# Attention heads taken two at a time, on the two halves of the array, in a three-block transformer kernel

## Time and profile before

| what | value |
|---|---|
| median of 3 runs | 1319.49 us (1318.44 to 1320.66) |
| the profiled execution, its own time | 1322.08 us |
| its span, first to last instruction | 1320.3 us |
| mean granted TensorE clock | 0.963 of 2.4 GHz |
| TensorE busy | 1267.0 us (96%) |
| VectorE busy | 850.8 us (64%) |
| ScalarE busy | 547.3 us (41%) |

### The profile page before, as it was taken

The page is one execution under the profiler, slowest core; times in us unless marked ns, Lnnn a source line. Parts: engine busy times, 40 slices in busy tenths (PEclk is TensorE's granted clock), DMA queues, the critical chain, the costliest instruction groups (busy, mean ns, idle before and its releaser), DMA issues.

```text
span 1320.3 us, 17461 instructions
## 1 busy us (share of the span) xinstructions
PE 1267.0 (96%) x7032; PEld 1074.1 (81%) x7032; DVE 850.8 (64%) x1314; ACT 547.3 (41%) x683; POOL 35.3 (3%) x43
## 2 busy tenths in 40 slices
PE   7999999999998999999999999989999999999996
PEld 5788777887997877777899888987877877999885
DVE  4565455446677788766777554675878766677542
ACT  5555454343433344443444333432344443434331
POOL 1121000000000000000000000000000000000000
PEclk9999999799998799999999999997899999999999
DMA  8456544236443322344455555452223444455540
GB/s 283 168 188 223 200 143 135 98 106 242 179 157 134 114 103 103 128 160 161 158 189 172 202 193 191 160 195 96 97 96 112 143 160 160 157 173 181 207 159 32
DMA packets 39468, 206.56 MB, mean 156 GB/s; under 512 B 4003, under 2 KB 13731, under 8 KB 16307
## 3 DMA queue, kind: packets, MB, share of 16 engines
q1 hardware_dynamic: 39052, 205.22, 44.7%
q10 hardware_dynamic: 336, 0.22, 0.1%
HBM read 204.23 MB, written 1.20 MB: 156 GB/s over the span
## 4 chain that ended last, share of the span: by engine, by line
PE 84%; DVE 9%; DVEq 2%; ACT 2%; issue 1%; DMA 0%; POOL 0%; POOLq 0%; ACTq 0%
PE panel L832 17%; PE panel L834 16%; PE panel L833 16%; PE panel L855 6%; PE panel L854 6%; PE panel L853 6%; PE tile L883 4%; DVE ring_parts L559 3%; PE heads_out L1034 2%; DVE area L1918 2%; PE tile L1161 1%; PE tile L1160 1%; DVEq L1919 1%; PE tile L1088 1%; PE tile L1086 1%
## 5 line engine op out<-in xcount | busy, mean ns | idle before, releaser
L559 DVE TENSOR_TENSOR ring_parts<-ring,ring_high 128x2048 fp32r<-128x2048 f32 (+1 forms) x185 | 415.3, 2257 | 169.3 <-ACT ring_high L534 151.5
L534 ACT ACTIVATE ring_high<-ring 128x2048 fp32r<-128x2048 f32 (+1 forms) x185 | 348.2, 1887 | 272.0 <-PE panel L834 205.0
L832 PE MATMUL panel<-ring_high,hT_high 128*128 128x512 f32 (+2 forms) x688 | 290.7, 423 | 11.6 <-DVE ring_parts L559 9.2
L834 PE MATMUL panel<-ring_high,hT_low 128*128 128x512 f32 (+2 forms) x688 | 272.4, 396 | 0.0
L833 PE MATMUL panel<-ring_parts,hT_high 128*128 128x512 f32 (+2 forms) x688 | 271.6, 395 | 0.0
L853 PE MATMUL panel<-hT_high,ring_high 128*128 128x256 f32 x704 | 199.4, 283 | 0.0
L855 PE MATMUL panel<-hT_high,ring_parts 128*128 128x256 f32 x704 | 199.2, 283 | 0.0
L854 PE MATMUL panel<-hT_low,ring_high 128*128 128x256 f32 x704 | 199.2, 283 | 0.0
L832 PEld LDWEIGHTS panel<-ring_high,hT_high 128*128 128x128 f32 x688 | 134.4, 195 | 55.8 <-issue 34.1
L832 PE MATMUL panel<-ring_high,area_parts 128*128 128x512 f32 x384 | 153.4, 399 | 5.0 <-DVE tok L1789 5.0
L834 PEld LDWEIGHTS panel<-ring_high,hT_low 128*128 128x128 f32 x688 | 134.0, 195 | 28.7
(11 more groups left out here) (225 smaller groups left out, 1256.3 us busy)
## 6 DMA issues: line engine op xcount, KB each, us to landing
ring<-in_w_layers_dram SPq DMA_DIRECT2D x140, 1024.0 KB, 4.9
ring<-in_w_first_dram SPq DMA_DIRECT2D x40, 1024.0 KB, 4.9
area<-bias_rows SPq DMA_DIRECT2D x16, 160.0 KB, 2.9
ring<-in_w_layers_dram SPq DMA_DIRECT2D x4, 560.0 KB, 3.8
area<-bias_rows SPq DMA_DIRECT2D x16, 96.0 KB, 2.9
area<-bias_rows SPq DMA_DIRECT2D x1, 1536.0 KB, 8.5
area<-in_gains_dram SPq DMA_DIRECT2D x3, 512.0 KB, 5.7
x<-in_x_dram SPq DMA_DIRECT2D x2, 512.0 KB, 4.3
```

The lines of the kernel that those rows point to most:

```text
L534: act.activation(ring_hi[:, hi, 0:w], ring[:, slot, 0:w], ACT.Copy).then_inc(high_ready, 1)
L559: g.tensor_tensor(ring_lo[:, slot, 0:w], ring[:, slot, 0:w], ring_hi[:, hi, 0:w], ALU.subtract).then_inc(low_ready, 1)
L832: pe.matmul(ps[:, b, 0:width], high, hi[:, k, :], start=first, stop=False)
L834: mm = pe.matmul(ps[:, b, 0:width], low, hi[:, k, :], start=False, stop=last)
```

## The change

Units are ordered in pairs of heads that lie on different halves of the array: in branch A and in the second blocks the order of heads becomes `PAIRS = [0, 4, 1, 5, 2, 6, 3, 7]`; in branch B neighbours already alternate. A score step now takes a pair, and in branch B one group g of it: the matmuls of the two heads alternate, into two PSUM tiles. The order of steps becomes: scores of the first pair; then for each pair T, T, scores of the next pair, V, V, and in the layers one empty slot. ScalarE's exponentials of unit u+2 stand at V(u). The columns of `heads_out`, the gates and outputs are addressed in the new order of heads, and the bias loads of the first block follow the pairs.

```diff
 def units_first():
-    return [("A", h, 1) for h in range(H)] + [("B", h, 2) for h in range(H)]
+    return [("A", h, 1) for h in PAIRS] + [("B", h, 2) for h in range(H)]
 def units_layer():
-    return [("s", h, 1) for h in range(H)] + [("w", h, 1) for h in range(H)]
+    return [("s", h, 1) for h in PAIRS] + [("w", h, 1) for h in PAIRS]
-def unit_steps(n):
-    out = [("S", 0)]
-    for u in range(n):
-        if u + 1 < n:
-            out.append(("S", u + 1))
-        out += [("T", u), ("V", u)]
+def pair_steps(units, spare):
+    def scores(p):
+        return [("S", p, g) for g in range(units[2 * p][2])]
+    pairs = len(units) // 2
+    out = scores(0)
+    for p in range(pairs):
+        out += [("T", 2 * p), ("T", 2 * p + 1)]
+        if p + 1 < pairs:
+            out += scores(p + 1)
+        out += [("V", 2 * p), ("V", 2 * p + 1)] + [None] * spare
     return out
-FIRST_PLAN = make_plan(FIRST_WIDE, unit_steps(2 * H), range(KC), {("mg2", 3): ["yA"]})
-LAYER_PLAN = make_plan(LAYER_WIDE, unit_steps(2 * H), (0, 1, 2, 3, 4, 5, 7), {
+FIRST_PLAN = make_plan(FIRST_WIDE, pair_steps(units_first(), 0), range(KC), {("mg2", 3): ["yA"]})
+LAYER_PLAN = make_plan(LAYER_WIDE, pair_steps(units_layer(), 1), (0, 1, 2, 3, 4, 5, 7), {
...
 # TensorE, first block
+            def scores_first(p, g):
+                pair = units[2 * p:2 * p + 2]
+                outs = [tile_for(part, score_tile(unit, g)) for unit in pair]
+                for b in range(NB):
+                    if pair[0][0] == "A":
+                        for i, (_, h, _) in enumerate(pair):
+                            r, c = head_rows(h)
+                            mm[i] = pe.matmul(outs[i][0][:, to], qaT[r, c, bs], kaT[r, :], start=True, stop=True)
...
 # TensorE, second blocks
+                        for i, (_, h, _) in enumerate(pair):
+                            r, c = head_rows(h)
+                            pe.matmul(outs[i][0][:, 0:P], qT[r, c, 0:P], kT[r, w, 0:P], start=True, stop=True)
+                        for i, (_, h, _) in enumerate(pair):
+                            r, c = head_rows(h)
+                            pe.matmul(outs[i][0][:, P:3 * P], qT[r, c, P:TOKENS], kT[r, w, :], start=True, stop=True)\
+                              .then_inc(outs[i][1], 1)
...
 # ScalarE (exp_layer likewise)
-                elif e == "S" and u == 0:
-                    exp_first(0)
+                elif e == "S":
+                    if u == 0:
+                        exp_first(0)
+                        exp_first(1)
-                elif e == "V" and u + 1 < len(units):
-                    exp_first(u + 1)
+                elif e == "V" and u + 2 < len(units):
+                    exp_first(u + 2)
...
 # VectorE
                 if e == "S":
-                    logits_first(u)
+                    for i in range(2):
+                        logits_group(2 * u + i, g)
...
 # sum_out, by b and in the new order of columns
-                e = v.tensor_tensor(y, y, two("yc").rearrange("p (b n) -> p b n", b=2)[:, :, hs_], ALU.add)
+                for b in range(NB):
+                    to = heads_of_group(y[:, b, :], i)
+                    e = v.tensor_tensor(to, to, heads_of_group(yc[:, b, :], i), ALU.add)
...
 # SyncE: bias of a pair of heads
-                            sp.dma_start(Es[odd:P:2, n % 2, i * TOEP:(i + 1) * TOEP], head_bias("A", 2 * n + i, odd))\
+                            sp.dma_start(Es[odd:P:2, n % 2, i * TOEP:(i + 1) * TOEP], head_bias("A", n + 4 * i, odd))\
```

More of the change, by code:

```diff
@@ L42 @@
 HALF = 4 * 512
+PAIRS = [0, 4, 1, 5, 2, 6, 3, 7]
 SLOTS = 6
@@ L145, in make_plan @@
             if s in slots and steps:
-                at.append(steps.pop(0))
+                step = steps.pop(0)
+                if step:
+                    at.append(step)
             plan[p, s] = at + [(e, 0) for e in extra.get((p, s), [])]
@@ L162, in plan_tiles @@
     for steps in plan.values():
-        for e, u in steps:
-            if e in "ST":
-                out += [f"{e}{units[u][0]}{units[u][1]}{g}" for g in range(units[u][2])]
+        for e, u, *g in steps:
+            if e == "S":
+                out += [score_tile(units[2 * u + i], g[0]) for i in range(2)]
+            elif e == "T":
+                out += [f"T{units[u][0]}{units[u][1]}{g}" for g in range(units[u][2])]
             elif e == "cmpS":
@@ L839, in rows_out @@
                         if plan:
-                            for e, u in plan[name, 4 * i + k]:
-                                step(e, u)
+                            for e in plan[name, 4 * i + k]:
+                                step(*e)
                         if 4 * i + k in after:
@@ L967, in head_rows @@
                 return slice(s, s + HD), h % 4
[L969 to L970 removed]
+            def scores_first(p, g):
+                pair = units[2 * p:2 * p + 2]
+                outs = [tile_for(part, score_tile(unit, g)) for unit in pair]
+                mm = [None, None]
                 for b in range(NB):
[L972 to L982, removed]
[L983 to L984 removed]
@@ L996, in turn_outputs, with step_first @@
                     turn(part, f"{('yA', 'yB')[t]}{b}", lambda c: y[:, b, c * P:(c + 1) * P])
-            def step_first(e, u):
+            def step_first(e, u, g=0):
+                if e == "S":
+                    if u == g == 0:
+                        for p in NORMED:
+                            for b in range(NB):
+                                wait_evicted(part, f"{p}{b}")
+                    scores_first(u, g)
+                    return
                 kind, h, n = units[u]
@@ new lines, in logits_group @@
+                mx, load = mxs[u % 2], bias_of(u)
+                if g == 0:
+                    v.wait_ge(E_loaded[load % 2], 64 * (load // 2 + 1) if kind == "A" else 32 * (load // 2 + 3))
+                    if u >= 2:
+                        k2, h2, n2 = units[u - 2]
+                        for g2 in range(n2):
+                            tile_of(v, part, f"T{k2}{h2}{g2}")
+                ps = tile_of(v, part, score_tile(units[u], g))
+                for b in range(NB):
+                    init = first[:, 12 + h:13 + h] if kind == "A" else low
+                    if g == 0:
+                        at = backwards(P * (1 - b), TOKENS, end=TOEP * (1 + (u % 2 if kind == "A" else 0)))
+                    else:
+                        at = backwards(0, TOKENS, end=5 * P)
+                    e = v.tensor_tensor_reduce(L[:, b, g * TOKENS:(g + 1) * TOKENS], ps[:, b * TOKENS:(b + 1) * TOKENS],
+                                               Es[:, load % 2, at], 1.0, init, ALU.add, ALU.max, mx[:, b, g:g + 1])
```

160 lines of the change are left out of this document (86 added, 74 removed).

## The result

| | before | after |
|---|---|---|
| median of the runs | 1318.97 us (4 runs, 1313.19 to 1320.66) | 1282.07 us (4 runs, 1281.08 to 1289.99) |
| the profiled execution | 1322.08 us | 1282.98 us |
| its span | 1320.3 us | 1281.2 us |
| mean granted clock | 0.963 | 0.975 |

The ratio is 0.974, 95% interval 0.969 to 0.979. The forecast was 1291 in a range of 1281 to 1304: right in sign and mechanism, 9 us too high, and one us from the range's lower end. The profiled executions differ by 39.1 us where the sum said 28.5. One kernel's time varies from execution to execution with the clock that it is granted: 49 more executions of the kernel before, made beside the experiments, took 1312.5 to 1323.0 us (median 1317.7), and ten of the kernel after 1281.0 to 1290.0 (median 1283.3), so that the medians differ by 34.4 and the profiled pair, with a slow one of before, by more.

What follows compares the result with a forecast made beforehand. TensorE was taken as the bound, busy 96%, with VectorE next in the layers. Terms summing to -28.5 took the profiled 1322.1 us to 1293.6; less 2.6 to the median, 1291 us, range 1281 to 1304.

Steps and rivals of the forecast that it cites:

- Points 1 to 3: Score steps taken in pairs: 5.0 us less in branch A, 7.0 in branch B, 16.8 less 1.8 in the layers.
- Points 4 and 5: Branch B: V10's 3.0 us wait for ScalarE goes, and the 13.66 us at half clock behind it, 6.3 us less.
- Point 6: First T, one chunk behind first scores, waits: 1.4 us in branch A, 2.4 and 1.0 in layers; 4.8 back.
- Point 7: VectorE in the layers, around the retention's normalisation: TensorE waits more for it, together 3.0 us back.
- does not come back: Rival: the low-clock stretch of branch B appears elsewhere, one or two more than forecast: 1297 to 1303 us; chance 0.18.
- one less: Rival: one low-clock stretch fewer, in the layers: 1285 us, or to 1281 with fewer waits; chance 0.08.
- Staggered starts: Rival: matmuls start in program order, so each score step lasts one instruction longer, 5.5 us: 1296 us; chance 0.08.
- One after the other: Rival: array halves do not overlap when both are wide, a pair saves only 0.40 us: 1308 us; chance 0.08.
- Late pairs: Rival: pairs' probabilities come late in the layers, TensorE waits at each pair's first T, 34 us: 1325 us; chance 0.06.

Runs made afterwards that it cites:

- both edits: The kernel after, with each layer's two runs of narrow compression matmuls cut in two and six convolution taps moved later: 1284.01 us, ratio 0.976.

## Why the prediction was right, and where its size was off

- **Points 1 to 3, the pair steps: right to 0.01 us.** 1.26, 1.29 and 1.05 measured. The halves do run at once, both wide, and whatever the order of issue; on one half the same instructions take 1.7 to 1.8 times as long (1.92 for 1.07, 1.50 for 0.86).
- **Points 4 and 5, V10: right.** No wait, and the granted clock is 1.00 from 197 to 246. The kernel before with only that wait shortened shows that the 13.66 us at half clock hung on it. The first block as a whole gained 19.5 us; the sum gives 5.0 + 7.0 + 3.0 + 6.3 - 1.4 = 19.9.
- **Point 6, the first T: right in place, a little high.** 1.30, 1.43 and 0.97 measured, 3.7 for 4.8. But it is not worth its length: the slot that took branch A's away gained nothing.
- **Point 7, VectorE: right in mechanism, low by 2.5 us.** The waits that hang on it rose by 5.5, not 3.0: those for exponentials from 2.6 to 7.1, less 2.4 at T0 which are point 6's, and 1.9 for T15's copy and 1.5 for a low part are new (7.1 - 2.4 - 2.6 + 1.9 + 1.5). The place was T12 and T13, as the checks named, with VectorE 85% busy in the stage. The stretch was worth 7.3 us between the profiled executions, as the moved taps show (1282.98 to 1275.64), which is more than its waits: probably the order gives the delay of a late T on, which no run separates.
- **The step that failed: the clock outside branch B, sized at nothing.** The sum let one stretch of 13.66 us go and left all others as they were. The time at half clock fell by 92.2 - 58.0 = 34.2 us. At the rate of point 5 (6.3 for 13.66) that is 15.8 us, 9.5 more than counted. The sum missed 10.6 us, and points 6 and 7 together went 1.4 the other way, so 12.0 are to be explained and some 2.5 stay unassigned. Part of this is the profiled pair's own luck: by the means over all executions the time at half clock fell by 26 us, which is 12 at the same rate and 5.8 more than counted, and the medians fell by 34.4, 5.9 more than the sum. The long stretches of the layers by window, first in the kernel before, then after, each under the wait at the first layer's entry:

```profile
403.22 0.77 PE L832 MATMUL panel<-ring_high,hT_high 128*128 128x512 f32 x1 [4.59 <-DVE ring_parts L559]
423.60:437.30 13.70, 13.70 (x47) 11.19 (x48) 3.94 (x14) 2.42 (x3) 0.00 (x0) 0.50 0.29 106
444.10:454.30 10.20, 10.20 (x38) 9.12 (x38) 8.29 (x28) 4.08 (x4) 0.00 (x0) 0.50 0.33 120
887.80:901.50 13.70, 12.34 (x30) 8.31 (x31) 10.72 (x22) 0.98 (x4) 0.00 (x0) 0.50 0.07 29
915.10:925.30 10.20, 10.20 (x33) 7.82 (x33) 3.17 (x12) 1.91 (x1) 0.00 (x0) 0.50 0.29 103
932.20:942.40 10.20, 10.20 (x40) 9.29 (x40) 8.15 (x29) 3.25 (x3) 0.00 (x0) 0.50 0.39 136
```

```profile
382.83 0.77 PE L874 MATMUL panel<-ring_high,hT_high 128*128 128x512 f32 x1 [4.59 <-DVE ring_parts L573]
380.70:387.50 6.80, 4.67 (x15) 3.01 (x16) 6.65 (x10) 0.56 (x1) 0.00 (x0) 0.50 0.24 101
404.50:414.70 10.20, 10.20 (x39) 9.13 (x39) 4.92 (x13) 2.40 (x2) 0.00 (x0) 0.50 0.46 173
425.00:428.40 3.40, 3.40 (x12) 2.82 (x12) 2.76 (x12) 0.87 (x2) 0.00 (x0) 0.50 0.54 142
861.90:868.70 6.80, 5.60 (x17) 3.75 (x18) 6.62 (x11) 0.00 (x0) 0.00 (x0) 0.50 0.10 41
885.80:892.60 6.80, 6.80 (x27) 6.02 (x27) 3.48 (x10) 2.09 (x2) 0.00 (x0) 0.50 0.46 158
902.80:909.60 6.80, 6.80 (x26) 6.03 (x25) 5.82 (x20) 2.73 (x3) 0.00 (x0) 0.50 0.46 157
```

Beside these there are stretches of 3.4 us, six before and five after. By place the 34.2 us are 13.7 at V10, nothing in the first layer (27.3 before and after: 3.4 us more at its start and 6.8 more in short stretches make up for 10.2 less at the narrow runs), 17.1 in the second (37.5 to 20.5) and 3.4 behind the planned panels. So the stretches at the narrow runs are shorter with pairs, but what a whole layer got back differs from layer to layer. Before and after, the stretches begin at the same kinds of place: in the runs of narrow compression matmuls, and around a wait of 4.6 us for a low part at the entry of each layer, which both kernels have. Behind or around this same wait there are, first and second layer, 3.4 and 13.7 us at half clock before, 6.8 and 6.8 after. The two halves at once are not the reason, since with both heads on one half the total is 51.2. What the pair order has in both is half as many score steps, and only V2 directly ahead of the second narrow run, where the kernel before had a score step (440.34). That this is the reason is argued, not shown.

- **The range and the rivals.** The clock was in the rivals from the wrong side: "does not come back" had 0.18, "one less" 0.08, and the latter is what happened, one and a half times over: 20.5 us besides V10's stretch. The result lies under the forecast's own range of 1285 to 1297, to which it gave 0.52, and inside the stated range only by the lower end that "one less, with fewer waits" had set; the waits of VectorE rose instead, so that the end came from a reason that did not happen. Staggered starts: refuted. One after the other: refuted by the traces, and the kernel on one half of the array shows what it would have cost. Late pairs: 5 to 6 us of waits, not 34; at most T steps there is none.
- **One check was badly put.** "Branch A's stretch to the first B score shorter by about 3.6" compares places that the new order moves: the first B score stands at slot 19 of the plan instead of slot 23. From the first A score to it are 49.95 us before and 40.42 after, and the difference is mostly chunks. The stage from S0 to the output is the fair one.

## What to carry to other kernels

When small matmuls of 64 rows stand between large ones, two of them on different halves of the array cost what one costs, in any order of issue; count what each saves from start to start, coming and going included. List the stretches at half clock first, each with its place, and give every one of them a term in the sum, if only a range: at V10, shortening a wait by 1.8 us took 10 us at half clock with it, elsewhere a wait of 2.9 us had none behind it. When TensorE gets faster beside a busy VectorE, look for work of VectorE without a near due time in the stretch where it is behind: six taps moved gave 7 to 9 us, a fifth to a quarter as much again as the change.

## What the runs showed of the hardware that was not expected

- Two heads' matmuls on different halves start 0.01 us apart in the records even when one head's four instructions all stand ahead of the other's in the program (step of 1.14 us for eight instructions, 1.99 on one half).
- A wait of 3.0 us (V10) was followed by 13.7 us at half clock and one of 1.2 at the same place by 3.4; one of 2.9 (ahead of the cut second run) by 17.1, and one of 1.3 at that place, in the kernel with both edits, by 13.6 in the first layer; one of 2.9 at a T step of the kernel with the empty slot by none in the next 17.7 us.
- A wait of 1.9 us at T13 has 3.4 us at half clock behind it in the first layer and none in the second, and one of 1.3 us (T0 of branch A) has none. So a wait's length alone doesn't say what follows.
- The estimated time at half clock of one and the same kernel differs by up to 29 us between executions (76 to 103 before, 49 to 77 after), and its time by some 10 us.
- Cutting a run of 5.3 us of narrow matmuls moved the time at half clock to the next run and left the sum within 3.4 us (58.0 and 54.6), which is less than it varies between executions.
